# The second branch's projection as a seven-product block scheme, with weight sums on GpSimd

## What is computed

```
branch_a = (gelu(lru_gate) * h) @ w_proj_a                   # (264 x 1024) @ (1024 x 1024)
y = (yg * ssd_norm)                                          # (264 x 2048)
branch_b = y @ w_proj_b                                      # (264 x 2048) @ (2048 x 1024)
merged = sigmoid(g_a) * branch_a + sigmoid(g_b) * branch_b
x = x + merged @ w_out                                       # then the experts
```

## Time and profile before

| | us |
|---|---|
| median of 3 runs (1350.51 to 1351.68) | 1351.16 |
| the profiled execution | 1351.37 |
| its span, first to last instruction | 1349.6 |
| TensorE busy (98%) | 1322.0 |
| weight loads of TensorE, beside it (54%) | 728.8 |
| VectorE busy (31%) | 417.4 |
| ScalarE busy (19%) | 260.5 |
| GpSimd busy (3%) | 37.6 |

### The profile page before, as it was taken

One profiled execution on the slowest core, in us unless ns is written; L12 is line 12 of the kernel. 1 busy time (PEld: TensorE's weight loads), 2 busy tenths in 40 slices (PEclk: granted clock), 3 DMA queues, 4 the chain that ended last, 5 costly groups with the idle time before them and its releaser, 6 DMA issues.

```text
span 1349.6 us, 16883 instructions
## 1 busy us (share of the span) xinstructions
PE 1322.0 (98%) x6850; PEld 728.8 (54%) x6850; DVE 417.4 (31%) x1090; ACT 260.5 (19%) x591; POOL 37.6 (3%) x60
## 2 busy tenths in 40 slices
PE   9999999999999999999989999998998999999998
PEld 7888888888887344343434434433343443444433
DVE  3755567795312221212112112121121121122112
ACT  2113374384202111010101101101010110101112
POOL 0000012110000000000000000000000000000000
PEclk9999999999999999999989999998998999999999
DMA  9445449898999999999999999999999999999996
GB/s 255 156 128 159 153 145 275 296 351 265 266 319 346 376 426 426 432 432 428 432 415 420 428 427 435 427 439 424 435 434 426 429 435 433 432 424 429 428 423 263
DMA packets 97930, 488.38 MB, mean 362 GB/s; under 512 B 9265, under 2 KB 74321, under 8 KB 77769
## 3 DMA queue, kind: packets, MB, share of 16 engines
q1 hardware_dynamic: 88032, 459.65, 84.5%
q0 software_dynamic: 4736, 24.44, 5.2%
q10 hardware_dynamic: 5113, 3.65, 1.0%
HBM read 476.78 MB, written 11.19 MB: 362 GB/s over the span
## 4 chain that ended last, share of the span: by engine, by line
PE 81%; DMA 17%; ACTq 1%; ACT 0%; SPq 0%; issue 0%; POOL 0%; DVE 0%; POOLq 0%; DVEq 0%
PE bank L330 79%; DMA ring<-in_w_gate_up 14%; DMA ring<-in_w_down 3%; PE bank L1023 2%; DMA plain_conv<-in_norm_mix 0%; SPq L399 0%; ACTq L734 0%; ACTq L732 0%; ACT exn L903 0%; POOL exn L645 0%; ACTq L655 0%; ACTq L659 0%; ACT plain_conv L989 0%; ACT plain_conv L884 0%; ACT ring L738 0%
## 5 line engine op out<-in xcount | busy, mean ns | idle before, releaser
L330 PE MATMUL bank<-ring,plain_conv 128*64 128x512 f32 (+1 forms) x1568 | 361.2, 603 | 17.3 <-DMA ring<-in_w_gate_up 17.3
L330 PE MATMUL bank<-exn,ring 128*128 128x264 f32 (+1 forms) x1168 | 262.2, 388 | 0.2 <-DVE exn L1619 0.2
L330 PEld LDWEIGHTS bank<-ring,plain_conv 128*64 128x64 f32 (+1 forms) x1568 | 111.1, 139 | 237.6 <-issue 215.1
L330 PEld LDWEIGHTS bank<-exn,ring 128*128 128x128 f32 (+1 forms) x1168 | 217.4, 189 | 40.3 <-issue 3.2
L330 PE MATMUL bank<-plain_conv 128*64 128x512 f32 (+2 forms) x592 | 126.9, 576 | 0.3 <-ACT ring L738 0.3
L2020 DVE TENSOR_SCALAR bank<-bank 128x512 f32<-128x512 f32 x31 | 21.7, 700 | 322.5 <-PE bank L330 322.5
L330 PE MATMUL bank<-ring,exn 128*64 128x512 f32 x512 | 120.5, 595 | 0.1
L2014 DVE TENSOR_TENSOR xT<-xT,bank 128x264 f32<-128x264 f32 x128 | 54.4, 429 | 211.0 <-PE bank L330 209.3
L330 PE MATMUL bank<-plain_conv,exn 128*64 128x512 f32 (+1 forms) x486 | 107.5, 591 | 0.5 <-DMA plain_conv<-in_w_down 0.4
L917 ACT ACTIVATE exn<-bank 128x512 f32<-128x512 f32 x31 | 18.5, 597 | 415.4 <-DVE bank L2020 415.4
L330 PEld LDWEIGHTS bank<-rstd,exn 128*128 128x128 f32 (+2 forms) x772 | 75.8, 190 | 15.5 <-issue 13.0
(11 more groups left out here) (308 smaller groups left out, 846.9 us busy)
## 6 DMA issues: line engine op xcount, KB each, us to landing
ring<-in_w_gate_up SPq DMA_DIRECT2D x24, 4096.0 KB, 22.7
ring<-in_w_gate_up SPq DMA_DIRECT2D x44, 2048.0 KB, 17.3
plain_conv<-in_w_gate_up SPq DMA_DIRECT2D x12, 4096.0 KB, 21.8
plain_conv<-in_w_down SPq DMA_DIRECT2D x11, 4096.0 KB, 26.7
ring<-in_w_down SPq DMA_DIRECT2D x11, 4096.0 KB, 29.7
ring<-in_w_in SPq DMA_DIRECT2D x36, 1024.0 KB, 5.4
plain_conv<-in_w_down SPq DMA_DIRECT2D x8, 2048.0 KB, 14.2
ring<-in_w_down SPq DMA_DIRECT2D x8, 2048.0 KB, 14.8
```

The costliest lines, as they stand in the source:

```text
L330: return nc.tensor.matmul(out, w, x, start=start, stop=stop)
```

## The change

Both halves are split in two: the 16 input tiles into tiles 0 to 7 and 8 to 15, the 264 tokens into 132 and 132, and the output tiles into neighbours (left = even, right = odd). For each of the four pairs of output tiles (`BLOCKS` = 4) the 2 x 2 x 2 block product is made by Winograd's form of Strassen's scheme: seven products of 8 matmuls with 132 columns, 28 products in all, where the plain form has eight. It needs sums of inputs (S1 to S4, once, on VectorE), sums of weights (T1, T2, one in place of the right chunk and T2 again, for each pair of output tiles, on GpSimd, 1024 elements on each partition) and sums of products (on VectorE, 132 elements each, after ScalarE has copied the first product out of PSUM). PSUM banks are used in pairs: `p_one, p_two, p_six, p_five`.

The order on TensorE is: products 1 and 2 of pair 0; then for each pair q: 5, 6, 3, (2 in q = 1 and 2), 7, product 1 of the next pair (or 2, in the last), 4. The third product waits on VectorE's `add_five`, the seventh on `add_six`, the fourth on `low_right`. In front of it all stands the last tile of the first projection, behind it the output projection, which takes its input tiles in the order 1, 0, 3, 2, ...

```diff
+        A11, A12, A21, A22 = [yT[:, KT * h:KT * h + KT, HT * i:HT * i + HT] for i in range(2) for h in range(2)]
+        S1, S2, S4, S3 = halves_of(8192), halves_of(T0 + 4224), halves_of(T0 + 5280), A21
+        p_one, p_two, p_six, p_five = [[ps[i], ps[4 + i]] for i in range(4)]
@@ SyncE @@
-                for c in range(D // width):
+                for c in (0, 1, 2, 3, 5, 4, 7, 6)[0:D // width]:
...
+                    if k == 2 * KT:
+                        free_at[s] = product_done[c // 2, 7 if c % 2 else 4]
...
-                        load_unit(0, 0)
-                    if k == 2 * KT and c == 7:
-                        load_unit(0, 1)
+                        load_half(0, 0, 0)
+                    if k == 2 * KT and c == 6:
+                        load_half(0, 0, 1)
+                        load_half(0, 1, 0)
+                    if k == KT and w is a["w_out"] and c == 1:
+                        load_half(0, 1, 1)
+            sp.wait_ge(S["acc_ready"], B_DONE)
             load_half(0, 4, 0)
-            sp.wait_ge(S["acc_ready"], 88)
+            sp.wait_ge(S["acc2_emptied"], 3 * BLOCKS)
             load_unit(0, 2)
@@ GpSimd @@
+            def sum_weights(q):
+                for c in (2 * q, 2 * q + 1):
+                    pool.wait_ge(landed[c % 4], 16 * (10 + c // 4) + 16)
+                left, right = stream[2 * q % 4], stream[2 * q % 4 + 1]
+                nc.gpsimd.tensor_tensor(T1[q % 2], right[:, 0:D], left[:, 0:D], ALU.subtract).then_inc(S["w_sum_ready"], 1)
+                pool.wait_ge(S["w_sum_ready"], 4 * q + 1)
+                nc.gpsimd.tensor_tensor(T2[q % 2], right[:, D:2 * D], T1[q % 2], ALU.subtract).then_inc(S["w_sum_ready"], 1)
+                nc.gpsimd.tensor_tensor(right[:, 0:D], right[:, D:2 * D], right[:, 0:D], ALU.subtract).then_inc(S["w_sum_ready"], 1)
+            def sum_weights_again(q):
+                pool.wait_ge(S["acc_ready"], product_done[q, 6])
+                pool.wait_ge(S["w_sum_ready"], 4 * q + 2)
+                nc.gpsimd.tensor_tensor(T2[q % 2], stream[2 * q % 4][:, D:2 * D], T2[q % 2], ALU.subtract).then_inc(S["w_sum_ready"], 1)
+            for q in range(BLOCKS):
+                if q > 1:
+                    pool.wait_ge(S["acc_ready"], product_done[q - 2, 4])
+                sum_weights(q)
+                sum_weights_again(q)
@@ ScalarE, behind the sigmoid (q = 0) and behind the small loads (q = 1 to 3) @@
+            def copy_first(q):
+                act.wait_ge(S["acc_ready"], product_done[q, 1])
...
+                nc.scalar.copy(p1_s[q % 2], p_one[q % 2][:, 0:HT]).then_inc(S["first_copied"], 1)
@@ TensorE @@
+            def third_product(q):
+                weights_landed(q, 1)
+                pe.wait_ge(S["part_taken"], 3 * q + 1)
...
+            def seventh_product(q):
+                pe.wait_ge(S["part_taken"], 3 * q + 2)
+                pe.wait_ge(S["w_sum_ready"], 4 * q + 3)
...
+            def fourth_product(q):
+                pe.wait_ge(S["part_taken"], 3 * q + 3)
+                pe.wait_ge(S["w_sum_ready"], 4 * q + 4)
@@ VectorE @@
+            for h in range(2):
+                done("y_sum_ready", V.tensor_tensor(S1[:, ks, :], A21[:, ks, :], A22[:, ks, :], ALU.add))
...
+            done("y_sum_ready", V.tensor_tensor(S2, S1, A11, ALU.subtract))
...
+            done("y_sum_ready", V.tensor_tensor(S4, A12, S2, ALU.subtract))
+            add_five(0)
+            done("y_sum_ready", V.tensor_tensor(S3, A11, A21, ALU.subtract))
+            add_six(0)
+            top_right(0)
             done("branch_gated", V.tensor_tensor(plain[:, GA:GA + KT, :], ...xnT..., ALU.mult))
-            for t in range(KT):
-                V.tensor_tensor(plain[:, GB + t, :], plain[:, GB + t, :], ps[t % 2][:, 0:NT], ALU.mult)
-                done("merged_ready", V.tensor_tensor(plain[:, GA + t, :], ..., ALU.add))
+            top_left(0)
+            low_right(0)
+            merge_right(0)
+            merge_left(0)
+            low_left(0)
+            merge_low_left(0)
+            for q in range(1, BLOCKS):
+                add_five(q)
+                add_six(q)
+                top_right(q)
...
```

More of the change, by code:

```diff
@@ L1194, in _, with project_a @@
                 in_tile(6 + t // 8, t % 8)
-            def project(g0, k_tiles, x_of, tiles0, first=0, end=8, ready=None):
-                per = 16 // k_tiles
+            def project_a(first, end):
                 for t in range(first, end):
-                    c, m = t // per, t % per
-                    s, n = c % 4, tiles0 + t
+                    s, m = t // 2, t % 2
                     if m == 0:
[L1202 to L1212, removed]
-                    ins.then_inc(S["acc_ready"], 1)
+                        pe.wait_ge(landed[s], 16 * 9 + 16)
+                    pe.wait_ge(S["acc_emptied"], 72 + t - 1)
+                    for k in range(KT):
+                        ins = mm(ps[t % 2][:, 0:NT], stream[s][:, 2 * P * k + P * m:2 * P * k + P * m + P], plain[:, GATE + k, :], k == 0, k == KT - 1)
+                    ins.then_inc(S["acc_ready"], 1)
@@ new lines, in project_out @@
+            def project_out(t):
+                s, m = t // 2, t % 2
+                if m == 0:
+                    pe.wait_ge(landed[s], 16 * 12 + 16)
+                if t > 1:
+                    pe.wait_ge(S["acc2_emptied"], 3 * BLOCKS + t - 1)
+                for n in range(KT):
+                    k = n ^ 1
+                    if t == 0 and n % 2 == 0:
+                        pe.wait_ge(S["merged_ready"], n + 1)
+                    if t == 0 and n % 2:
+                        pe.wait_ge(S["merged_ready"], n + 1)
+                    ins = mm(ps[t % 2][:, 0:NT], stream[s][:, 2 * P * k + P * m:2 * P * k + P * m + P], plain[:, GA + k, :], n == 0, n == KT - 1)
+                ins.then_inc(S["acc_ready"], 1)
@@ new lines, in weights_of, with weights_landed, multiply @@
+            def weights_of(q, right):
+                c = 2 * q + right
+                return stream[c % 4]
+            def weights_landed(q, right):
+                c = 2 * q + right
+                pe.wait_ge(landed[c % 4], 16 * (10 + c // 4) + 16)
+            def multiply(bank, w, x, ready=None):
+                for k in range(KT):
+                    if ready:
+                        pe.wait_ge(*ready(k))
+                    ins = mm(bank[:, 0:HT], w[:, P * k:P * k + P], x[:, k, :], k == 0, k == KT - 1)
+                ins.then_inc(S["acc_ready"], 1)
@@ L1405, in second_half @@
                     if isinstance(j, int) and j in SPLIT[c]:
-                        pe.wait_ge(half_landed[c], 16 * ((len(SPLIT[c]) + more) * p + SPLIT[c].index(j) + 1 + more))
+                        pe.wait_ge(half_landed[c], 16 * ((len(SPLIT[c]) + more) * p + SPLIT[c].index(j) + 1 + (more and not first)))
                     elif c in halves and not isinstance(j, int):
@@ L1627, in _ @@
             link(V.tensor_scalar(lt[1], lam, -1.0, None, ALU.mult))
-            done("lam_abs", V.tensor_tensor(lt[1], lt[1], lam, ALU.max))
+            done("exp_in", V.tensor_tensor(lt[1], lt[1], lam, ALU.max))
             def log1p(e, s, s2, p):
@@ L1728, in _ @@
             link(V.tensor_tensor(wdec[:, 0, :], last[:, 0, :], tok[:, 2, :], ALU.subtract))
-            done("wdec_in", V.tensor_tensor(wdec[:, 1, :], wdec[:, 0, :], last[:, 1, :], ALU.add))
+            done("exp_in", V.tensor_tensor(wdec[:, 1, :], wdec[:, 0, :], last[:, 1, :], ALU.add))
             for t in range(LX, NCONV):
@@ L1868, in _, with add_five, add_six @@
             done("yr_ready", V.reciprocal(y_rms, y_rms))
+            def add_five(q):
+                dve.wait_ge(S["acc_ready"], product_done[q, 5])
+                dve.wait_ge(S["first_copied"], q + 1)
+                done("part_taken", V.tensor_tensor(p15, p1_s[q % 2], p_five[q % 2][:, 0:HT], ALU.add))
+            def add_six(q):
+                dve.wait_ge(S["acc_ready"], product_done[q, 6])
+                link(V.tensor_tensor(p16, p1_s[q % 2], p_six[q % 2][:, 0:HT], ALU.add))
+                dve.wait_ge(S["part_taken"], 3 * q + 1)
+                done("part_taken", V.tensor_tensor(p15, p15, p_six[q % 2][:, 0:HT], ALU.add))
```

181 lines of the change are left out of this document (143 added, 38 removed).

## The result

The changed kernel takes 1358.70 us (median of 4 runs, 1358.63 to 1359.05) against 1350.93 for the kernel before, run beside it: a ratio of 1.0056, 95% interval 1.0042 to 1.0070. It is 7.8 us slower where the prediction had it 3.8 us faster, and 4.2 us above the upper end of its range. The profiled execution took 1358.74 us, its span 1357.0.

The account below looks back on a forecast made before the run. TensorE was taken to bound the second projection (56.96 us). Its new length, 50.85 + 0.3 + 0.8 + 1.2 = 53.15 us, a gain of 3.8, gave a median of 1347.4 us, range 1345.4 to 1354.5.

Parts of the forecast that it names:

- TensorE's part: Second projection: 448 records of 132 columns at 0.1135 us, 50.85 us in place of 56.96, a gain of 6.1.
- The first waits: Block 0 of the projection: TensorE waits 0.3 us for product 6 and 0.8 us for product 4.
- GpSimd's price: Weight sums of 1024 elements on GpSimd: 1.9 us each, with 1.8 and 3.6 as ends.
- merges in pairs: Block 0's merges on VectorE pass two at a time between GpSimd's sums; product 3 of block 1 waits 1.2 us.
- rival C: Merges and GpSimd's sums alternate one for one; product 3 of block 1 waits 5.2 to 5.5; 1354.2 us; chance 0.20.
- clock term: In rival C, the long wait puts TensorE's clock to 0.50; the 80 records behind it take 2.65 us more.
- Rival D: GpSimd goes on without a break; product 4 of blocks 0, 1, 2 each 2 to 3 us late; 1351.7; chance 0.18.
- Rival B: Ports no hindrance for VectorE operations of 0.3 to 0.4 us; projection 51.5 us, gain 5.5, 1345.7; chance 0.12.
- The weights' order: Chunk 4 lands at 365.4 us, just in time for product 1 of block 2 at 366.5; up to 1 if late.
- The experts: A projection that ends x us sooner starts the experts' full weight stream x us sooner.
- E: Gain made and given back, by late chunks (4 or 6) or a weight stream not starting sooner; 1350.5; chance 0.10.

## Why the prediction was wrong

**TensorE's part: right.** Without waits three products take 5.40 us in the kernel with the sums on VectorE (348.25 to 353.65), 1.80 each or 0.1125 us a record, for 0.1135 in the prediction and inside 0.1113 to 0.1146. 28 x 1.80 = 50.4 us, and the first four products lose 0.53 in small steps (7.73 us for 7.20): 50.93 for 50.85.

**The first waits: right in place, small.** Of that 0.5, 0.26 stand behind the start of product 5, where the prediction had 0.3 in front of product 6, and 0.27 in front of product 5 (344.39 for 344.12), where it had nothing. Product 4 of block 0 waited 0.42 for 0.8. The gate began at 350.40, waited out the rest of the sum under way and took 2.87 us for 2.36; the next sum, begun at 351.02, stood still until the gate was done and took 4.46 us.

**GpSimd's price: mis-sized.** 1.9 us was assumed, half of the 3.64 of the earlier trace rows; it is 2.34 to 2.36 where nothing holds it. The prediction put the difference to broadcast inputs in the earlier trace rows and added 0.1 us for it. That cannot be the whole reason: the 16 sums added to the kernel before have broadcast inputs too and took 2.36 us (their median). Why the operation of the earlier trace rows was cheaper is open. The estimate from the Trainium skill, "GPSIMD Engine Reference", section "3.1 Elementwise — side-by-side cycle accounting", 2.25 us, was nearer. Alone, at 2.25, it would have moved the forecast from a gain of 3.8 to one of 2.6, as the text had it; it did not turn the sign.

**The step that failed: merges in pairs.** From VectorE's 0.03 us between dependent operations and GpSimd's 0.24 after a dependence the prediction took it that VectorE gets two merges through between two sums. The trace shows one for one: behind the first, five merge operations of 2.1 to 2.5 us, each ending with a sum. A gap between dependent instructions says how soon an engine can ask, not who is served. GpSimd's next sum was asking already: of the four sums of block 1 the second depends on the first, yet it started at 355.56, 0.08 us after the first's end, so the 0.24 of the earlier trace rows was not even the gap. This is rival C, given 0.20. Its formula, 4x - 2.1, gives 7.3 us for x = 2.35; measured 7.95. That it comes so near is in part luck, for it counts four whole sums behind the first, each with a merge of 0.4 us added. The six operations in fact passed five, and these start only 2.30 to 2.51 us apart (2.31 to 2.44 where no merge was held), so a merge between two sums adds at most 0.2 us. Its clock term, 2.65 from the earlier trace rows, was 1.83 behind this wait (9.19 for 7.36). C at x = 2.35 would have been 50.85 + 0.3 + 0.8 + 7.3 + 2.65 = 61.9 us; measured 63.2. What it left out is the wait of 1.12 us in block 2. The prediction gave VectorE time to recover there and counted nothing, but two merges of block 2 met the first two sums of block 3.

As a sum for the changed kernel: 50.93 + waits 9.49 + slower records 2.31 (1.83 at the long wait, 0.37 and 0.11 at the two short ones; of the 0.37, 0.27 are one more small wait, of product 6 of block 1 for the sum that ended at 357.99) + 0.5 at their edges = 63.2. (The waits are counted from the end of the record before them; records that follow without a wait overlap by 0.16 us, and three such overlaps are gone.)

**Rival D**, GpSimd without a break, is out: between any two of the six sums shown one merge was served. **Rival B**, no hold for operations so short, is out as well, by 1.55 to 2.47 us for 0.29 to 0.43. **The weights' order** was right: TensorE shows no wait for a chunk in any of the seven-product kernels. **The experts** follow the start of the stream, as predicted; of 6.2 us later the end is 7.4 later. **E** has its small part in this, since the fast versions also give something back: the sums on VectorE start the experts 6.06 us sooner and end 5.6 us sooner.

The range took in C only at x = 1.9, 1354.2 us. Of the 4.5 us from there to 1358.7, 3.2 stand in the projection (63.2 for 60.0), where a sum of 2.35 us and the wait in block 2 were missing, and 1.2 in the experts, for which C had nothing. With 2.25 us a sum, as the text had it beside C, the time was about 1355.5: still 3.2 short. A gain as large as B's was there (5.6 us of span for 5.5), with the sums on the engine that the change had spared.

## What to carry to other kernels

Work moved to GpSimd was not free for VectorE here, though GpSimd had nothing else to do. Count each VectorE operation with two SBUF inputs as taking the rest of a GpSimd operation on top, one for one, and look at what queues behind it. Then give such an operation one input in PSUM, or do the work on VectorE if it has the time; here the first, and the second with some steps reordered, each turned a loss of 7.8 us into a gain of 5 to 6. When a forecast rests on who is served first, put the other order's full price in the range.

## What the runs showed of the hardware

- VectorE and GpSimd operations with two SBUF inputs each alternated one for one while both had work. The one that came second waited for about the rest of the other: merges of 0.29 to 0.43 us took up to 2.54, and a sum of 2.34 us begun during the gate took 4.46. The Trainium skill, "SBUF — State Buffer", "SBUF: two separate sides", names the shared ports; who is next when both wait is what these rows add.
- A VectorE operation with one input in PSUM was not held in any of these traces: 0.28 to 0.30 us for 132 columns and 0.43 to 0.44 for 264 with a sum beside it.
- A float32 sum of 1024 columns took 2.34 us on GpSimd and 1.22 on VectorE.
- The clock was still 1.00 at 361 to 364 us, with TensorE idle since 360.11, and 0.50 at 367 to 370. After a wait of 7.95 us the next 64 records took 1.83 us more than usual, after one of 4.66 the next 32 took 1.62 more; after the wait of 1.12 us the next 48 took 0.11 more, with the clock at 1.00.
- Matmuls of 132 columns with full-width float32 weights have a distance of 0.1125 us, little above the 0.110 of 32 columns.
